# Routing inside the output projection: router logits from the first sublayer's sum, one block's selection beside the next block's products

## The reference, cut to what matters

```
x   = x + gt1 * rmsnorm(concat(conv_out, att) @ w_out, g_post1)
h   = rmsnorm(x, g_pre2) * (1 + sc2) + sh2          # a2 = g_pre2 (1 + sc2), b2 = sh2
g_prob = softmax(h @ w_rg + b_rg);  g_top, g_idx = top_k(g_prob, 1)
e_sel  = (h @ w_re + b_re)[the 8 experts of group g_idx]
e_top, e_idx = top_k(softmax(e_sel), 2);  e_w = e_top / sum(e_top) * g_top
out = sum over the two experts e of  e_w * (silu(h @ w_gate[e]) * (h @ w_up[e])) @ w_down[e]
x   = x + gt2 * rmsnorm(out, g_post2)
```

## Time and profile before

| what | us |
|---|---|
| runs | 726.66, 729.72, 861.23; median 729.72 |
| the profiled execution, and its span | 726.36, 724.6 |
| TensorE products busy | 589.2 (81%), 3118 instructions |
| VectorE, ScalarE, GpSimd busy | 258.9, 148.6, 84.8 |
| mean granted clock of TensorE | 0.943 of full speed |
| memory read, written | 161.48 MB, 17.06 MB |

### The profile page before, as it was taken

One profiled execution on the slowest core, in us unless ns is written; L12 is line 12 of the kernel. 1 busy time (PEld: TensorE's weight loads), 2 busy tenths in 40 slices (PEclk: granted clock), 3 DMA queues, 4 the chain that ended last, 5 costly groups with the idle time before them and its releaser, 6 DMA issues.

```text
span 724.6 us, 8142 instructions
## 1 busy us (share of the span) xinstructions
PE 589.2 (81%) x3118; PEld 308.6 (43%) x3119; DVE 258.9 (36%) x445; ACT 148.6 (21%) x298; POOL 84.8 (12%) x103
## 2 busy tenths in 40 slices
PE   0889899999999999989999348878998787778800
PEld 0656565655555455544455223333433233323400
DVE  2316899999442143312233540100110100000134
ACT  3220000012315444322223202100011000001233
POOL 5000000600000000001111035111111111110002
PEclk9999999999999999999999759989999999989965
DMA  9999926000008430044214921599999999999468
GB/s 334 344 374 383 357 89 231 14 0 1 0 1 326 176 145 1 1 152 196 117 58 185 395 71 31 197 413 410 424 424 425 425 426 426 425 426 428 202 268 187
DMA packets 49269, 171.79 MB, mean 237 GB/s; under 512 B 5722, under 2 KB 14267, under 8 KB 36938
## 3 DMA queue, kind: packets, MB, share of 16 engines
q1 hardware_dynamic: 41216, 156.11, 53.9%
q0 software_dynamic: 6736, 13.59, 6.1%
q10 hardware_dynamic: 1274, 1.52, 0.6%
HBM read 161.48 MB, written 17.06 MB: 246 GB/s over the span
## 4 chain that ended last, share of the span: by engine, by line
PE 60%; DMA 23%; DVE 5%; issue 3%; ACT 3%; PEldq 1%; PEld 1%; SPq 1%; DVEq 0%; ACTq 0%; POOLq 0%; POOL 0%
DMA arena<-in_w_up 14%; PE ps L1273 14%; PE ps L1457 10%; PE ps L1521 9%; DMA arena<-in_w_ada 6%; PE ps L1432 5%; PE ps L1534 4%; PE ps L1278 4%; PE ps L1274 4%; PE ps L1441 3%; PE ps L1291 2%; DMA arena<-h_d,idg 2%; PE ps L1357 2%; PE ps L1411 1%; ACT arena L870 1%
## 5 line engine op out<-in xcount | busy, mean ns | idle before, releaser
L1521 PE MATMUL ps<-arena 128*64 128x512 f32 x512 | 120.1, 622 | 22.1 <-DMA arena<-in_w_up 16.4
L1273 PE MATMUL ps<-arena 128*128 128x512 f32 x256 | 132.0, 597 | 1.2 <-issue 1.2
L998 DVE SCALAR_TENSOR_TENSOR arena<-arena 128x655 f32<-128x655 f32 x116 | 95.0, 897 | 0.4 <-issue 0.2
L1521 PEld LDWEIGHTS ps<-arena 128*64 128x64 f32 x512 | 44.8, 143 | 96.2 <-issue 92.2
L1278 PE MATMUL ps<-cst,arena 128*128 128x128 f32 (+2 forms) x349 | 54.0, 298 | 33.1 <-DVE arena L937 17.4
L1534 PE MATMUL ps<-arena 128*64 128x512 f32 x272 | 63.5, 609 | 16.3 <-ACT arena L870 15.8
L1274 PEld LDWEIGHTS ps<-arena 128*128 128x128 f32 x256 | 48.7, 190 | 61.5 <-issue 61.5
L1457 PE MATMUL ps<-arena 128*128 128x512 f32 x160 | 69.2, 593 | 0.9 <-ACT arena L822 0.9
L1278 PEld LDWEIGHTS ps<-cst,arena 128*128 128x128 f32 (+2 forms) x349 | 44.7, 178 | 50.8 <-issue 42.4
L1221 DVE TENSOR_TENSOR arena<-arena,ps 128x256 f32<-128x256 f32 x16 | 6.7, 421 | 129.6 <-ACT arena L875 117.2
L1274 PE MATMUL ps<-arena 128*128 128x128 f32 (+1 forms) x256 | 50.9, 280 | 0.0
(11 more groups left out here) (242 smaller groups left out, 519.9 us busy)
## 6 DMA issues: line engine op xcount, KB each, us to landing
arena<-in_w_gate SPq DMA_DIRECT2D x16, 2048.0 KB, 19.6
arena<-in_w_up SPq DMA_DIRECT2D x16, 2048.0 KB, 25.4
arena<-in_w_down SPq DMA_DIRECT2D x16, 2048.0 KB, 30.2
arena<-in_w_ada SPq DMA_DIRECT2D x12, 2048.0 KB, 13.8
arena<-y_d SPq DMA_DIRECT2D x10, 512.0 KB, 7.1
arena<-in_w_in SPq DMA_DIRECT2D x8, 512.0 KB, 12.3
arena<-in_w_out SPq DMA_DIRECT2D x1, 4096.0 KB, 12.6
arena<-ada_d SPq DMA_DIRECT2D x8, 512.0 KB, 10.1
```

The costliest lines, as they stand in the source:

```text
L998: ins = dve.scalar_tensor_tensor(dst, src, w, dst, ALU.mult, ALU.add)
L1273: mm(pp(name)[:, 0:TS], lhs(k), rhs_s(k), start=k == 0, stop=k == steps - 1)
L1521: last = mm(ps[a:a + ROWS, s, :], src[:, k, a:a + ROWS], slots[w][:, j, 0:2, k * FE:(k + 1) * FE], start=k == 0, stop=k == KD - 1)
```

## The change: what it does

* The router's logits are no longer made of h2. Since h2 = x · r · a2 + b2 (r the reciprocal root of a token), h2 @ wr = r · (x @ (a2 wr)) + (b2 @ wr), so TensorE turns x itself (`ht{b}`), multiplies the turned columns as weights with `wr` scaled by a2 (36 columns moving, `lg_ps`), and VectorE applies r and adds a bias row. `wr0` is the scaled matrix of the prompt, `wr` that of the sample. The order of the router weights' rows changes with it: x is turned in plain slices (`(k p)` in place of `(p k)`).
* For that, four rows of the modulation are turned early (`turn34`, between q1 and q2), b2 @ wr is made (`rb`, after `cache`), GpSimd scales `wr` and makes two diagonals, and ahead of the output projection TensorE spreads the two bias rows over the partitions (`small`), which VectorE copies (`bias_ready`).
* Between the products of `P{b}` now stand, for the block before, the turning (after 6 products), the logits (after 9) and the positions (after 15), and after 12 the part of `table0` of block b − 2. VectorE selects block by block (`route`, `find`), ScalarE makes the numbers (`numbers`). PSUM slots are given by `HOME`: P alternates between 0 and 1, ht has 3, small results have 2.
* The last block's projection goes half by half, and its norm, sum, turning and logits are split in two halves.
* Table 0 adds the padding in its own product and is finished in PSUM; table 1 stands on TensorE behind it, ahead of pair 0. The counts' wait moves behind pair 0's down products.
* GpSimd gathers pair 3's rows in pair 0's turn. Buffers `ys`, `xg`, `xT` are laid out anew. SyncE loads the down pieces of pairs 1 and 2 only when pair 1's gather is in.
* The root's scaling and epsilon go into ScalarE's instruction; adding to x takes one VectorE instruction (two products of the norm before it take one each).

The diff, cut to its core:

```diff
-POST = ["P0", "P1", "P2", "ht0", "P3", "rt0", "ht1", "P4", "rl0", "rt1", "ht2", "ht3", "rl1", ...]
+POST = ["small", "P0", "P1", "ht0", "P2", "ht1", "P3", "ht2", "P4", "ht3", "ht4"]
+HOME = {"small": 2, **{f"P{b}": b % 2 for b in range(NT)}, **{f"ht{b}": 3 for b in range(NT)}}
...
             landed(sp, f"P{NT - 1}")
-            load_pair(2, 2)
-            sp.wait_ge(h2_last, 1)
+            load_pair(2, 2, pieces=range(2))
+            sp.wait_ge(h2_ready, NT)
+            sp.wait_ge(xg_in[1], 16)
             load_pair(1, 1, pieces=range(2, 3))
+            load_pair(2, 2, pieces=range(2, 3))
...
+            emptied(gp, "rb")
+            gp.wait_ge(proj_dve, 1)
+            gp.tensor_tensor(wr0, wr[:], a2T[:, :, 0:1].broadcast_to([P, KD, G + E]), ALU.mult)
+            gp.tensor_tensor(wr[:], wr[:], a2T[:, :, 1:2].broadcast_to([P, KD, G + E]), ALU.mult)
...
-                if 0 < pair < PAIRS - 2:
+                if pair == 0:
+                    gp.wait_ge(e_tr, 2)
+                    gather(xg[:, 1, :], idg[:, 0, 3:4], xg_in[1])
+                elif 1 < pair < PAIRS - 2:
                     gp.wait_ge(e_tr, pair + 1)
                     gather(xg[:, s, :], idg[:, 0, pair + 2:pair + 3], xg_in[s])
...
-            act.dma_start(x_rg, i["w_rg"][0].rearrange("(p k) e -> p k e", k=KD)).then_inc(wr_in, 16)
+            act.dma_start(x_rg, i["w_rg"][0].rearrange("(k p) e -> p k e", p=P)).then_inc(wr_in, 16)
...
             dve.wait_ge(a2_in, 32)
             dve.wait_ge(b2_in, 32)
+            dve.wait_ge(bias_in, 1)
+            dve.tensor_copy(biasrow, bias_ps).then_inc(bias_ready, 1)
...
+            def route(b):
+                dve.wait_ge(lg_done, b + 1)
+                step(dve.scalar_tensor_tensor(L, lg_ps[:, b, :], stat[:, 7, b:b + 1], biasrow[:, v, :], ALU.mult, ALU.add))
+                first_best(pen, Lg, hitg, best0, rankg, 1e30)          # 4 steps
+                step(...)                                               # em
+                first_best(oh[:, 0, b, :], em, hit, best1, ranke)
+                step(...)
+                first_best(oh[:, 1, b, :], em, hit, best2, ranke)
+                dve.tensor_scalar(rt_e[:, b, 0:G], Lg, best0, None, ALU.subtract).then_inc(mask_ready, 1)
...
+            begin(pe, "small")
+            pe.wait_ge(wr2_ready, 1)
+            for v in range(2):
+                last = mm(bias_ps[:, v, :], ones[0:G + E, :], diag[:, v, :], start=True, stop=True)
+            last.then_inc(bias_in, 1)
             pe.wait_ge(wo_in, 16)
+            pe.wait_ge(bias_ready, 1)
+            for b in range(NT):
...
+                for n, (k, half) in enumerate(steps):
+                    if b and n == 6:
+                        turn_rows(b - 1)
+                    if b and n == 9:
+                        if b >= 2:
+                            pe.wait_ge(place_ready, b - 1)
+                        logits(b - 1)
+                    if b >= 2 and n == 12:
+                        table(0, b - 2)
+                    if b and n == 15:
+                        places(b - 1)
+                    last = mm(pp(name)[:, half * 512:(half + 1) * 512], mixT[:, k, b * P:(b + 1) * P], ...)
+            turn_rows(NT - 1)
+            pe.wait_ge(place_ready, NT - 1)
+            table(0, NT - 2)
+            logits(NT - 1)
+            places(NT - 1)
+            pe.wait_ge(place_ready, NT)
+            table(0, NT - 1)
+            ...
+            pe.wait_ge(place_ready, NT + 1)
+            for b in range(NT):
+                table(1, b)
```

More of the change, by code:

```diff
@@ L630, in expert_pair @@
                     gp.wait_ge(e_ysb, 1)
[L631 removed]
+                scatter(ys[s], ids[:, 0, pair:pair + 1], y_st[s])
                 if pair == 0:
@@ L1161, in places @@
                 last.then_inc(place_ready, 1)
-            places(0)
-            dve.tensor_tensor(wide(8), oh1, table, ALU.mult)
-            step(dve.tensor_tensor(wide(9), oh2, table, ALU.mult))
-            for c in range(2):
-                dve.tensor_reduce(base[:, c, :].unsqueeze(2), wide(8 + c), AX.X, ALU.add)
-            step(dve.tensor_copy(rnd_i, at))
-            dve.tensor_scalar(rnd_i, rnd_i, ROWS.bit_length() - 1, None, ALU.arith_shift_right)
-            step(dve.scalar_tensor_tensor(base, at, float(PAIRS), base, ALU.mult, ALU.add))
@@ new lines, in _ @@
+            find(NT - 2)
+            b = NT - 1
+            name = f"P{b}"
+            dve.wait_ge(pss, NT + 1)
+            dve.tensor_tensor(po[:, 512:], pp(name)[:, 512:], gg1[:, 1, 512:], ALU.mult)
+            dve.wait_ge(psd, NT)
+            step(dve.reciprocal(stat[:, 5, b:b + 1], stat[:, 5, b:b + 1]))
+            for half in range(2):
+                part_ = slice(512 * half, 512 * (half + 1))
+                ins = dve.scalar_tensor_tensor(x[:, b, part_], po[:, part_], stat[:, 5, b:b + 1], x[:, b, part_], ALU.mult, ALU.add)
+                if half:
+                    free(ins, name)
+                    dve.drain().then_inc(x1_ready, 1)
+                else:
+                    ins.then_inc(x1_ready, 1)
@@ L1384, in _ @@
             done(last, "cache")
+            emptied(pe, "turn34")
+            pe.wait_ge(wr_ready, 1)
+            begin(pe, "rb")
+            for k in range(KD):
+                last = mm(pp("rb")[0:G + E, 0:2], wr[:, k, :], b2T[:, k, :], start=k == 0, stop=k == KD - 1)
+            done(last, "rb")
             emptied(pe, "kr")
@@ new lines, in logits, with places @@
+            def logits(b):
+                if b == NT - 1:
+                    pe.wait_ge(xT_half, 1)
+                else:
+                    emptied(pe, f"ht{b}")
+                for k in range(KD):
+                    if b == NT - 1 and k == KD // 2:
+                        emptied(pe, f"ht{b}")
+                    last = mm(lg_ps[:, b, :], x1T[:, k, :], (wr if b else wr0)[:, k, :], start=k == 0, stop=k == KD - 1)
+                last.then_inc(lg_done, 1)
+            def places(b):
+                pe.wait_ge(mask_ready, b + 1)
+                steps = [(trib if a == b else onesb, c, a) for a in range(b + 1) for c in range(2)]
+                for n, (w, c, a) in enumerate(steps):
+                    last = mm(pos_ps[:, b, :], w[:], oh[:, c, a, :], start=n == 0, stop=n == len(steps) - 1)
+                last.then_inc(pos_done, 1)
@@ new lines, in _ @@
+            turn_rows(NT - 1)
[5 more added lines that the diff above has]
+            table(0, NT - 1)
+            for a in range(NT):
+                for c in range(2):
+                    last = mm(cnt_ps, onesb[:], oh[:, c, a, :], start=a == c == 0, stop=a == NT - 1 and c == 1)
+            last.then_inc(cnt_done, 1)
+            pe.wait_ge(place_ready, NT + 1)
```

449 lines of the change are left out of this document (237 added, 212 removed).

## The result

| what | before | changed |
|---|---|---|
| median, lowest and highest of 7 runs each | 729.72, 726.66, 861.23 | 733.48, 732.54, 736.09 |
| ratio of the runs, 95% interval | | 1.0067 [1.0049, 1.0086] |
| profiled execution, its span | 726.36, 724.6 | 736.09, 734.3 |
| TensorE products busy | 589.2 | 600.6 |
| mean granted clock of TensorE | 0.943 | 0.932 |

The changed kernel is 0.67% slower, 4.9 us of 729.7 (interval 3.6 to 6.3). The forecast was 734.2 and "within 2%". The two profiled executions lie further apart, 9.7, since that of before is at the low end of its runs and that of the changed kernel is the highest of its seven. The run of 861.23 stands far from the six others of its kernel (726.66 to 730.09) and is not in the ratio.

What follows compares the result with a forecast made beforehand. It took full transfer engines from the fourth pair's load as the bound, with only their start movable. −16.15 + 7.5 + 3.1 + 10.1 + 0.3 + 1.5 + 1.5 = +7.9 on 726.36 gave 734.2; own range 730 to 738.

Steps and rivals of the forecast that it cites:

- T: The end of the last block's products, where ScalarE starts on them; 391.27 in the kernel before.
- ahead of attention: turn34, rb, packets: Before attention: four more transpositions and eight products cost +1.5, the router weights' small transfer pieces +1.5.
- wait ahead of block 0: Before block 0's output products: TensorE waits for the bias copy, which stands behind a2 and b2; +7.5.
- clock in block 0: In block 0: the clock falls in the pause and six us at half rate lose 3; +3.1.
- inserted work and its stall: Blocks 1 to 4: work between products adds 14.1, less 4.0 removed, +10.1; a stall from block 0's table load, +0.3.
- after T, to pair 0: Behind the last block: only one block left to select, so pair 0 starts at T + 19.0 instead of T + 35.15; −16.15.
- the wall: From pair 3's load: thirteen pairs' weights go through full transfer engines; only its start can move, its length not.
- the 42 short products just ahead of pair 0: The second table's products in TensorE's queue, ready at T + 17.3 and taking 1.5, so pair 0 starts at T + 19.0.
- some 11: Sign ahead of block 0: the first output product comes some 11 us after the last attention product.
- 0.32 from which selection would have outlasted its cover: Rival, blocks and after T: selection steps take 0.40, not 0.25; +7.6, giving 742; decides from 0.32 a step; chance 0.13.
- the rival: After T: the last h2 store takes 8.5 to land and delays the gather; +3.3, giving 737.5; chance 0.10.
- The rival in which TensorE counts in pairs 2 and 3: Pairs 2 and 3: removing the stall before 485 is worth 5.9, giving 728; chance 0.09.

Runs made afterwards that it cites:

- The two experiments: Changed kernel with the bias row copied before VectorE's waits: 0.9961 of the kernel before; kernel before with TensorE made to wait for a2 and b2: 1.0133.
- the kernel of doubled logits: Changed kernel with the logits of blocks 0 to 3 made twice, the second set overwriting the first: 1.0188 of the kernel before.
- the kernel with the early copy and idle products: Changed kernel with the bias row copied before VectorE's waits and 22 idle TensorE products behind the last block's products: 0.9893 of the kernel before, median 722.62.
- the kernel before with the added wait: Kernel before, with TensorE made to wait for a2 and b2 ahead of block 0's first product: 1.0133, +9.7 us.
- the gather experiment: Changed kernel with pair 3's gather put back in pair 1's turn of GpSimd: 1.0099 of the kernel before.
- both kernels with idle products: Changed kernel with early bias copy and 22 idle products: 0.9893 of the kernel before; the same with all pair 2's weights loaded behind pair 1's gather: 0.9922.
- the early-copy kernel: Changed kernel with VectorE's copy of the bias row put ahead of its waits for gg1, a2 and b2: 0.9961 of the kernel before.
- the one with the old order of down pieces: Changed kernel with SyncE's loads of pair 1's and 2's weights ordered as before the change, not waiting for the gather: 1.0159 of the kernel before.

## Why the prediction was right, step by step

The mechanism held: a gain after T, a loss ahead of it that is larger, and transfers that pass on what is left. In numbers, from the two profiles:

| step | forecast | profiles |
|---|---|---|
| ahead of attention: turn34, rb, packets | +3.0 | +1.0 |
| clock in attention's last products | | +1.4 |
| wait ahead of block 0 | +7.5 | +8.0 |
| clock in block 0 | +3.1 | +2.4 |
| inserted work and its stall | +10.4 | +9.0 |
| after T, to pair 0 | −16.15 | −13.75 |
| pair 0 to pair 3's load | 0 | −0.4 |
| the wall | 0 | +1.4 |
| behind it | 0 | +0.6 |
| sum | +7.9 | +9.7 |

That the sum is near is in part luck. Terms taken too large (4.5 in all: ahead of attention, block 0's clock, inserted work, pair 0) and terms taken too small or not at all (6.3: after T, the wait, attention's clock, the wall, behind it) cancelled. And as a difference from the kernel before, +7.9 lies outside the measured 3.6 to 6.3; the forecast time, 734.2, is only 0.7 off the median because it was counted from an execution that stands 3.4 under the median of before.

Of the signs that the prediction named, the pause, the low clock into block 0, the 42 short products just ahead of pair 0 and the full transfers came; the blocks lie 16.5 to 17.1 apart, at and under the lower edge of 17.0; the first output product came 8.9 after the last attention product, near the prediction's own pause of 8.4 and not the "some 11" of its signs; and the gather at T + 16.7 misses its 13 to 15.

**After T** is the term that was off most. The logits were taken at the 1.9 of the warm clock (3.63, and their end at T + 8.2 instead of 6.2); the clock, which the prediction weighed for block 0, was not weighed here. The 16 steps took 4.85, so 0.30 each and not 0.25: above the assumption, but below the 0.32 from which selection would have outlasted its cover, and so blocks 1 to 4 show no stall. The store was issued at T + 9.2 as forecast but took 6.6 to land, not 3.8: the rival had the direction, and 0.4 of its 3.3, since the ids were late too. The second table did not stand in the way; TensorE had it done at 433.9, before the rows were in.

**The wait and its clock** were sized right in kind and sum (10.6, profiles 10.4). The wait was 0.5 longer; the clock was back 4.8 after the restart and not after 6, which is 2.4 and not 3.1. The two experiments put them at 7.7 and 9.7 in the time.

**Inserted work** was 9.0: the logits 1.7 to 1.8 a set and not 1.9, places and table short. The pace is that of loads of 128 columns, and the kernel of doubled logits shows it to be paid in full. By the Trainium skill, "TensorE: Matmul & The Clock Gate" (LDWEIGHTS), 16 loads of 128 columns are 1.7, an estimate from its 107 ns; the 1.70 to 1.8 here agree at 2.4 GHz. At 1.2 GHz the set took 3.63, twice that; the formula given there has no clock in it, and the measurement decides.

**Ahead of attention** the pair of profiles has 1.0 of the forecast's 3.0, and the packets look overrated. From 15 to 27 us ScalarE's queue moved 2147 packets, 1789 more than before:

```profile
q10 hardware_dynamic: 2147, 0.16, 12.4%
```

12.4% less 4.6% of 12 us is 0.94 of all engines, not 2.8, and the vector chunk at 84 us landed when it had before (84.05, 83.87). The 1.0 is seen on the load of `w_out` (245.59, 246.63) and fits turn34 and `rb`. But one pair of executions is too few here. No experiment's edit touches anything ahead of that load, and it stands at 245.9 to 248.8 in the eight profiles of the changed kernel and its variants (mean 247.5), and at 244.8 and 245.6 in the two of the kernel before. So the term is anything from 0.3 to 4.0, some 2.2 on the mean, and 3.0 is not refuted. Five of those eight also show TensorE waiting for a modulation load near 80 us (0.2 to 1.4), which neither profile of the kernel before does. The packets alone were not tried, so their share is open.

**The clock in attention** has nothing to do with the change as far as is known. Its last projection runs at half rate in the changed kernel, here from 313.83, 3.34 for four passes:

```profile
313.83 4.63 PE L1513 MATMUL ps<-arena 128*128 128x512 f32 x7 [0.90 <-ACT arena L867]
```

It took 5.92 where before took 4.53. The changed kernel's second profile, the kernel with the early copy and idle products and the kernel before with the added wait show it as well, the other five kernels and the kernel before do not.

**The wall** grew by 1.4, though its transfers stay full (1.01 and 425 GB/s, as in the earlier trace rows). One of its last loads was late and TensorE's clock low behind it; 32 passes that took 7.1 at this place before took 10.05:

```profile
669.02 10.05 PE L1638 MATMUL ps<-arena 128*64 128x512 f32 x32 [4.04 <-DMA arena<-in_w_up]
```

Over all the experiments' profiles the wall was between 231.6 and 235.9 long, so 1.4 is within what one execution shows against another. The sign "if the wall's length changes" is met by no more than that. The rival in which TensorE counts in pairs 2 and 3 at its full 5.9 fell with the gather experiment; a smaller share is not ruled out.

Between the 9.7 of the profiles and the 4.9 of the runs, 1.4 in attention and 1.4 in the wall can be put down to single executions; what is then left, some 2 us, is not settled. The runs of the changed kernel alone spread over 9 us.

## What to carry to other kernels

When a wait is added on a fast path, look at what the releasing engine itself waits for first: here a copy of 0.23 us stood behind two transfers it did not need, and moving two lines was worth 7.7 us. Work put between products of the engine that sets the pace is paid in full. Swapping operands so that the narrow one moves gained nothing: 16 float32 passes took 1.87 with 128 columns of weights and 36 moving, and 1.94 the other way round before. Short products behind a wait ran at the low clock here, so such a chain of latencies is to be summed at the low rate. Idle products kept the clock up into pair 0 and the kernel came out another 5 us faster, of which a part may be a late start in the kernel that it is compared with.

## What was not expected of the hardware

* A store of 512 KB took 2.6 us with no load beside it and 6.5 to 7.0 with 4 MB of loads issued some 9 us earlier. It took 9.3 with 6 MB issued up to 9 us earlier and 2 MB issued beside it.
* Rows gathered took 4.6 with no loads beside them and 7.9 beside loads.
* Behind the first doubled set of logits the clock fell to 1.2 GHz for 4 us, although TensorE shows no gap in products there (busy 2.00 of 2.00 from 358 to 360). Behind the other three doubled sets, and behind the single sets of blocks 0 to 3, it did not fall. Behind the last block's set it fell for some 3 us in both kernels with idle products (0.50 from 411 to 414 in the first), again with TensorE busy.
* The third step of the last selection on VectorE (4 columns, 0.22 us in the blocks before) ended 0.01 to 0.02 us after GpSimd's addition of `b2` in all eight profiles of the changed kernel and its variants, whenever it had begun: 0.33 us long in the changed kernel, 1.68 and 1.63 with the idle products. That the addition holds the step is inferred from these ends; no run moved the addition away.
* ScalarE began its first copy of pair 0's extra round 1.3 us after the turned rows were ready in the early-copy kernel and 2.1 us after in the one with the old order of down pieces, where it took 0.04 in the one with idle products. VectorE's copy beside it was 2.3 and 3.0 us late. The profile names nothing that they waited for.
